# A ring of eight places: keeping the split weights of one token half for the other

## The chip, the cores and the metric

The kernel runs on one core of a Trainium2 chip. The metric is the device time of one execution, in microseconds (us). TensorE is called PE here, VectorE DVE, ScalarE ACT, GpSimd POOL, and SP is the engine that issues nearly all loads.

## The reference, cut to what matters

One token sequence (512 tokens, 1024 features, plus 256 context tokens later) goes through two layers of a first block and two layers of a second. Everything is float32. The change touches the first block, whose layer is

```
f = swiglu(modulate(x, sh1, sc1), ffn_in[l, 0], ffn_out[l, 0])
x = deepnorm_residual(x, f, g1, ln_g[l, 0], ln_b[l, 0], 0.5)
u = modulate(x, sh2, sc2)
m = even_mixer(u, ...)   # l = 0: RG-LRU and gated linear attention
m = odd_mixer(u, ...)    # l = 1: latent attention with low-rank q, k, v
x = deepnorm_residual(x, m, g2, ln_g[l, 1], ln_b[l, 1])
f = swiglu(modulate(x, sh3, sc3), ffn_in[l, 1], ffn_out[l, 1])
x = deepnorm_residual(x, f, g3, ln_g[l, 2], ln_b[l, 2], 0.5)
```

`deepnorm_residual` is a residual sum followed by a layer norm over the 1024 features of each token.

## The kernel before, in words

**Products.** Features lie on the partitions, tokens along the free axis. A weight matrix is cut into slabs: a slab is 128 output columns by up to 8 tiles of 128 input rows, 128 x 1024 numbers, 512 KB. For float32 accuracy each product is made of three: the weight is split into a high part (fp32r) and a low part (the rest), and so is the activation; PE adds high x high, high x low and low x high (L644 to L646), 24 matmuls for a slab. `class Lin` is one product (name, tensor, slabs, who makes the low parts), `SLABS` the list of all slabs in the order of use.

**The way of a slab.** SP loads it into one of `NRAW` = 3 raw places (`sp_slabs`, L526); it waits until the slab three before it has its low part. ACT copies it to the high part (`act_slabs`, L558). DVE ("v") or POOL ("g") subtracts to make the low part (`low_slabs`, L568); a name such as "vg" means by turns. High and low part lie in a split place (`halves`, L504): places 0, 1, 2 of 2048 words each, for some products also 3 and 4 (`place_slabs`, L215). A slab may be written to its place when the slab before it there (`before`) has had its last matmul (`release`).

**Token halves.** Where a product stands next to a layer norm, it is made in two passes, A for tokens 0 to 255 and B for tokens 256 to 511, so that the norm of one half runs beside the matmuls of the other. These are `gu` (l, f, 0, "A"/"B"), the first 8 slabs of `ffn_in`; `fo` (l, f, 1, A/B), the second half of `ffn_out`, whose slabs are in two parts (768 and 640 columns); `ob` and `oo`, the last products of the mixers, and `oi`, the first product of the odd mixer, of 4 slabs. Each pass loads and splits its slabs anew. gu(l, f) is used below for the pass pair of layer l, feed-forward f.

**Order.** Every engine's instructions are written out by a Python generator and run in that order. For output group m of a product, the engine first does the split work up to slab `ahead(m)` (L59), then its own work for m (`epilogue`): `act_linear`, `dve_linear`, `pool_linear` (L679 to L696). `ahead(m)` is the last slab whose place is free once the slabs before m have been used; with five places that is four slabs on. SP goes three further (`loads`).

**The seam between two passes.** In a tail pass (`fo`, `ob`, `oo`) DVE adds the residual for each m (L977), ACT squares it (L1071), POOL sums the tiles (L1048) and the squares (L1078). After the first slab of the next pass PE adds these sums over the partitions (`pe_ln`, L1098); DVE and ACT make mean and scale from them (`dve_ln` and `act_ln` at m = 0: L1149 to L1159, L1128), which stand in the queues behind the split work of m = 0; in the middle of its second slab PE spreads them over the partitions (`pe_ln_spread`, L1108). Then DVE normalizes two tiles per m (L1167, L1171, L1180), ACT writes the high part (L1131), DVE the low part (L1143) of the next product's input. At the start of `oo` ACT and POOL split the attention output (L1784, L1838).

Of the kernel before, what the change touches and what calls it, by code (L numbers as in the profile page):

```python
# [45 lines left out]
class Lin:  # L46


    def __init__(self, name, tensor, idx, mgs, kt, k0, mt, kch, split, low, toks):
# [4 lines left out]
        self.slab0 = 0  # L54
# [4 lines left out]
    def ahead(self, m):  # L59

        last, n = self.first(m) + len(self.cuts) - 1, self.first(m)

        def room(i):
            plain = i >= NRAW and not SLABS[i - NRAW].lin.split and i - NRAW >= last
            return not plain and (SLABS[i].before is None or SLABS[i].before < last)

        while n + 1 < len(SLABS) and room(n + 1):
            n += 1
        return n
# [54 lines left out]
def low_in(name):  # L124
    return {"B": "vg"}.get(name[-1], "v")
# [5 lines left out]

def weight_plan():
    out = []

    def lin(name, tensor, idx, mgs, kt=8, k0=0, mt=1, kch=8, split=True, low="v", toks=0):
        out.append(Lin(name, tensor, idx, mgs, kt, k0, mt, kch, split, low, toks))

    def ffn(l, f):
        for half in range(2):
            for name, tile0, cols in ffn_parts(l, f, half):  # L140
                n = 8 if len(name) > 4 else 22 - 2 * tile0
                lin(name, "ffn_in", (l, f), range(22 * half + 2 * tile0, 22 * half + 2 * tile0 + n), low=low_in(name))
# [23 lines left out]
    for name in ab("ob"):  # L166
        lin(name, "even_out", (), range(8), k0=8, low=low_out(name))
    ffn(0, 1)
    ffn(1, 0)
    for name in ab("oi"):  # L170
        lin(name, "odd_in", (), range(4), low=low_in(name))
# [4 lines left out]
    for name in ab("oo"):  # L176
        lin(name, "odd_out", (), range(8), low=low_out(name))
# [24 lines left out]
for _x in PLAN:  # L202
    _x.slab0 = len(SLABS)
# [10 lines left out]

def place_slabs():  # L215
# [3 lines left out]
    for n, s in enumerate(SLABS):  # L219
        if s.lin.split:  # L220
            more = [3, 4] if s.lin.name[0] in ("gu", "fo", "ob") or s.lin.name == ("oo", "B") else []
            ring = [0, 1, 2] + (more or ([5] if s.lin.name == ("glu", 0) else []))
            i = (i + 1) % len(ring)
            s.slot, s.before = ring[i], holds.get(ring[i])
            holds[ring[i]] = n
# [102 lines left out]
def _build(nc, a, out, ctx):  # L328
# [84 lines left out]
    scale_w = [ar(o, o + D) for o in SCALE_AT]  # L413
    HH, HL = rregion(F0, 11, 512)
# [89 lines left out]
    def halves(n):  # L504
        o, w = (SPL0, SPL0 + 2048, SPL0 + 4096, MORE0, MORE0 + 2048, E3)[SLABS[n].slot], SLABS[n].c1 - SLABS[n].c0
# [40 lines left out]
    def act_slabs(upto):  # L546
        while to_split["a"][0] <= min(upto, len(SLABS) - 1):
# [8 lines left out]
            if s.slot in (3, 4) and s.lin.name[0] == "ob":  # L556
                se.wait_ge(*(yield "p_gs", 3))
            se.activation(halves(n)[0], raw(n), ACT.Copy).then_inc(*sig("a_hi", n))  # L558
# [2575 lines left out]
```

## Time and profile before

| | us |
|---|---|
| median of 3 runs | 3929.87 (3925.76 to 3931.29) |
| the profiled execution | 3930.48 |
| its span | 3929.2 |
| PE busy | 3712.5 (94%) |
| DVE busy | 2164.7 (55%) |
| ACT busy | 1479.0 (38%) |
| POOL busy | 1082.3 (28%) |

The span is the time from the first to the last instruction of the profiled execution; the 1.3 us that the execution's own time is above it lie outside the program's instructions. Busy time of different engines overlaps. Times in the rows below are us from the span's start.

### The profile page before, as it was taken

How to read it: one execution, taken by the hardware profiler on the slowest of the kernel's cores; microseconds unless marked ns; L12 is line 12 of the kernel's file. 1: busy time of each engine (PE TensorE's matmuls, PEld its weight loads, DVE VectorE, ACT ScalarE, POOL GpSimd, SP SyncE). 2: the span in 40 equal slices, each digit the busy share in tenths (PEclk: the TensorE clock that was granted, in tenths of full speed). 3: DMA queues.
4: the chain of work that ended last, by engine and by line, in shares of the span. 5: the costliest groups of instructions: out<-in, count | busy, mean ns of one | idle time of the engine just before them, and what ended most of it. 6: DMA issues, size and time to landing. Idle time of an engine off the chain costs nothing.

```text
span 3929.2 us, 53436 instructions
## 1 busy us (share of the span) xinstructions
PE 3712.5 (94%) x21052; PEld 3105.7 (79%) x21052; DVE 2164.7 (55%) x3761; ACT 1479.0 (38%) x2556; POOL 1082.3 (28%) x753
## 2 busy tenths in 40 slices
PE   8999999899999999889999899899999989799999
PEld 7889878798889888659878777678778877677777
DVE  6555784675667776646333588821155338840442
ACT  3223554452235223444323423432235323353352
POOL 0003103251014102205201422933211423354224
PEclk9999999999999999998999899899999999899999
DMA  7565334345755565304332311012111212112112
GB/s 297 170 202 168 129 104 149 110 141 179 238 180 172 168 196 162 104 22 141 117 104 88 117 53 56 33 44 68 46 38 33 65 43 81 59 49 94 57 44 97
DMA packets 132153, 433.94 MB, mean 110 GB/s; under 512 B 14784, under 2 KB 14912, under 8 KB 131520
## 3 DMA queue, kind: packets, MB, share of 16 engines
q1 hardware_dynamic: 131904, 430.52, 33.8%
q8 instruction: 169, 2.77, 0.3%
q14 instruction: 80, 0.66, 0.1%
HBM read 428.36 MB, written 2.10 MB: 110 GB/s over the span
## 4 chain that ended last, share of the span: by engine, by line
PE 77%; DVE 11%; issue 5%; ACT 3%; POOL 3%; DMA 1%; SPq 0%; DVEq 0%; ACTq 0%; POOLq 0%
PE ps L644 21%; PE ps L646 21%; PE ps L645 21%; DVE cut L2287 4%; PE ps L1981 2%; POOL cut L568 1%; POOL cut L1048 1%; PE ps L1858 1%; PE ps L1942 1%; PE ps L1958 1%; PE ps L1964 1%; PE ps L642 1%; PE ps L1946 1%; DVE cut L568 1%; PE ps L670 1%
## 5 line engine op out<-in xcount | busy, mean ns | idle before, releaser
L644 PE MATMUL ps<-cut 128*128 128x512 f32 (+1 forms) x5312 | 1877.4, 353 | 88.9 <-DVE cut L2150 18.4
L645 PE MATMUL ps<-cut 128*128 128x512 f32 (+1 forms) x5312 | 1853.1, 349 | 0.0
L646 PE MATMUL ps<-cut 128*128 128x512 f32 (+1 forms) x5312 | 1851.8, 349 | 0.0
L644 PEld LDWEIGHTS ps<-cut 128*128 128x128 f32 x5312 | 1020.2, 192 | 245.6 <-issue 84.9
L645 PEld LDWEIGHTS ps<-cut 128*128 128x128 f32 x5312 | 1021.7, 192 | 127.6 <-issue 5.1
L646 PEld LDWEIGHTS ps<-cut 128*128 128x128 f32 x5312 | 1019.9, 192 | 126.8
L558 ACT ACTIVATE cut<-cut 128x1024 fp32r<-128x1024 f32 (+3 forms) x680 | 633.4, 939 | 840.7 <-PE ps L646 707.8
L568 POOL TENSOR_TENSOR cut<-cut 128x1024 fp32r<-128x1024 f32 (+3 forms) x266 | 580.9, 2186 | 1308.7 <-ACT cut L558 1308.3
L568 DVE TENSOR_TENSOR cut<-cut 128x1024 fp32r<-128x1024 f32 (+3 forms) x414 | 506.6, 1226 | 429.6 <-ACT cut L558 429.5
L945 POOL TENSOR_TENSOR cut<-cut 128x512 fp32r<-128x512 f32 (+1 forms) x100 | 143.8, 1438 | 1094.1 <-ACT cut L904 1094.1
L2287 DVE SCALAR_TENSOR_TENSOR cut<-cut,cols 128x512 f32<-128x512 f32 (+1 forms) x330 | 282.7, 857 | 11.7
L581 DVE CUSTOM_DVE_ANT_0 cut<-cut,cols 128x1024 f32<-128x1024 f32 x128 | 171.1, 1337 | 19.0 <-DMA cut<-in_mod_w 17.1
L926 DVE TENSOR_TENSOR cut<-cut,ps 128x512 f32<-128x512 f32 (+1 forms) x100 | 62.1, 621 | 186.3 <-PE ps L646 186.1
L2007 ACT ACTIVATE cut<-cut,st 128x512 f32<-128x512 f32 (+2 forms) x160 | 110.8, 694 | 137.6 <-DVE st L2040 137.5
L899 ACT ACTIVATE cut<-ps 128x512 f32<-128x512 f32 (+1 forms) x100 | 54.3, 543 | 271.4 <-PE ps L646 271.4
L2455 DVE TENSOR_TENSOR cut<-cut,ps 128x512 f32<-128x512 f32 (+1 forms) x48 | 28.0, 597 | 228.1 <-PE ps L646 228.1
L1048 POOL TENSOR_TENSOR cut<-cut 128x256 f32<-128x256 f32 x84 | 77.9, 927 | 153.1 <-DVE cut L977 153.1
L977 DVE SCALAR_TENSOR_TENSOR cut<-ps,deriv,cut 128x256 f32<-128x256 f32 (+1 forms) x144 | 81.5, 566 | 28.9 <-PE ps L646 28.9
L2299 POOL TENSOR_SCALAR const<-cut,cols 128x256 f32<-128x256 f32 x90 | 84.6, 940 | 8.6
L1981 PE MATMUL ps<-cut 128*64 128x128 f32 x1216 | 83.4, 280 | 0.7 <-DVE cut L2057 0.7
L904 ACT ACTIVATE cut<-cut 128x512 fp32r<-128x512 f32 (+1 forms) x100 | 56.8, 568 | 64.2 <-DVE cut L926 64.2
L589 DVE CUSTOM_DVE_ANT_0 cut<-cut,cols 128x1024 f32<-128x1024 f32 x48 | 79.7, 1661 | 1.7
(323 smaller groups left out, 3491.6 us busy)
## 6 DMA issues: line engine op xcount, KB each, us to landing
cut<-in_ffn_in SPq DMA_DIRECT2D x200, 512.0 KB, 4.1
cut<-in_mod_w SPq DMA_DIRECT2D x136, 512.0 KB, 4.4
cut<-in_ffn_out SPq DMA_DIRECT2D x96, 384.0 KB, 3.4
cut<-in_ffn_out SPq DMA_DIRECT2D x96, 320.0 KB, 3.2
cut<-in_w_ada SPq DMA_DIRECT2D x48, 512.0 KB, 3.5
cut<-in_w_merge SPq DMA_DIRECT2D x48, 512.0 KB, 3.5
cut<-in_even_in SPq DMA_DIRECT2D x36, 512.0 KB, 3.6
cut<-in_proj SPq DMA_DIRECT2D x48, 256.0 KB, 2.6
```

Source lines behind the costliest of these rows:

```text
L558: se.activation(halves(n)[0], raw(n), ACT.Copy).then_inc(*sig("a_hi", n))
L568: engine.tensor_tensor(lo, raw(n), hi.bitcast(F32), ALU.subtract).then_inc(*sig(which + "_lo", n))
L581: ve.tensor_tensor_reduce(junk, w, cb, 1.0, col("mod_b", 72 * l + i), ALU.mult, ALU.add, modc[:, 72 * l + i:72 * l + i + 1]).then_inc(*sig ...
L644: te.matmul(o, hi[:, k - ka, w], xs[0], start=k == 0, stop=False)
L645: te.matmul(o, hi[:, k - ka, w], xs[1], start=False, stop=False)
L646: ins = te.matmul(o, lo[:, k - ka, w], xs[0], start=False, stop=last)
L945: ge.tensor_tensor(HL[:, t, g[0]:g[1]], FTMP[t % 2][:, g[0]:g[1]], HH[:, t, g[0]:g[1]].bitcast(F32), ALU.subtract).then_inc(*sig("g_hl", g ...
L1048: ge.tensor_tensor(total, total if m > 1 else XA[:, 0, g[0]:g[1]], XA[:, m, g[0]:g[1]], ALU.add).then_inc(*sig("g_total", tag, part[-1], m))
L1981: ins = te.matmul(PS[b][64 * s:64 * s + 64, 0:128], J["v"][s][k], pbuf[:, s, k * 128:(k + 1) * 128], start=k == 0, stop=k == nv - 1)
L2007: se.activation(x, x, ACT.Exp, bias=stat(i, 1, s), accum_out=stat(i, 2, s)).then_inc(*sig("a_exp", tag, i, s))
L2287: ve.scalar_tensor_tensor(out=o, in0=x, scalar=c, in1=o, op0=ALU.mult, op1=ALU.add).then_inc(*sig("v_tap", l, t, h0, j))
L2299: ge.tensor_scalar(tmp, i, w, None, ALU.mult).then_inc(*sig("g_tmp", l, x, j))
```

## The change

B passes of `gu`, `ob`, `oi` and `oo` take the slabs of their A pass (`again`), which stay in their places until B has used them; they are not loaded or split a second time. So that a pass has room for 8 slabs, some lie in places beside the ring ("side"): free parts of the buffer at that time. The slabs in side places may be written when the last slab of the product before has been used (`before` = the slab ahead of the product's first). `oi` now has the ring of five, `oo` a ring of three and five side places, `gu` and `ob` a ring of five and three side places. During B a ring place comes free with each used slab, and the next product's slabs go there. The low parts of all these slabs are made by DVE. `fo` keeps its two passes as they were.

```diff
--- before.py
+++ after.py
@@ -46,12 +46,12 @@
 class Lin:
 
 
-    def __init__(self, name, tensor, idx, mgs, kt, k0, mt, kch, split, low, toks):
+    def __init__(self, name, tensor, idx, mgs, kt, k0, mt, kch, split, low, toks, again):
         self.name, self.tensor, self.idx, self.mgs, self.kt, self.k0 = name, tensor, idx, list(mgs), kt, k0
         self.mt, self.kch, self.split, self.low, self.toks = mt, kch, split, low, toks
         self.cuts = [(ka, min(kt, ka + kch)) for ka in range(0, kt, kch)]
         self.groups = len(self.mgs) * mt
-        self.slab0 = 0
+        self.slab0, self.again, self.stays = 0, again, False
 
     def first(self, m):
         return self.slab0 + (m // self.mt) * len(self.cuts)
@@ -59,10 +59,14 @@
     def ahead(self, m):
 
         last, n = self.first(m) + len(self.cuts) - 1, self.first(m)
+        end = self.slab0 + len(self.mgs) * len(self.cuts)
+        if self.again:
+            n = end - 1
 
         def room(i):
             plain = i >= NRAW and not SLABS[i - NRAW].lin.split and i - NRAW >= last
-            return not plain and (SLABS[i].before is None or SLABS[i].before < last)
+            freed = self.slab0 if self.stays and i >= end else last
+            return not plain and (SLABS[i].before is None or SLABS[i].before < freed)
 
         while n + 1 < len(SLABS) and room(n + 1):
             n += 1
@@ -122,24 +126,29 @@
 
 
 def low_in(name):
-    return {"B": "vg"}.get(name[-1], "v")
+    return "v"
 
 
 def low_out(name):
     return {"A": "v", "B": "gv"}.get(name[-1], "v")
 
 
+def first_of(name):
+
+    return name[:-1] + ("A",) if name[-1] == "B" else None
+
+
 def weight_plan():
     out = []
 
-    def lin(name, tensor, idx, mgs, kt=8, k0=0, mt=1, kch=8, split=True, low="v", toks=0):
-        out.append(Lin(name, tensor, idx, mgs, kt, k0, mt, kch, split, low, toks))
+    def lin(name, tensor, idx, mgs, kt=8, k0=0, mt=1, kch=8, split=True, low="v", toks=0, again=None):
+        out.append(Lin(name, tensor, idx, mgs, kt, k0, mt, kch, split, low, toks, again))
 
     def ffn(l, f):
         for half in range(2):
             for name, tile0, cols in ffn_parts(l, f, half):
                 n = 8 if len(name) > 4 else 22 - 2 * tile0
-                lin(name, "ffn_in", (l, f), range(22 * half + 2 * tile0, 22 * half + 2 * tile0 + n), low=low_in(name))
+                lin(name, "ffn_in", (l, f), range(22 * half + 2 * tile0, 22 * half + 2 * tile0 + n), low=low_in(name), again=first_of(name))
             for name in ([("fo", l, f, 0)], ab("fo", l, f, 1))[half]:
                 lin(name, "ffn_out", (l, f), range(8), kt=11, k0=11 * half, kch=6, low=low_out(name))
 
@@ -164,17 +173,17 @@
     for m in range(8):
         lin(("g", m), "even_in", (), [24 + m], low="g")
     for name in ab("ob"):
-        lin(name, "even_out", (), range(8), k0=8, low=low_out(name))
+        lin(name, "even_out", (), range(8), k0=8, again=first_of(name))
     ffn(0, 1)
     ffn(1, 0)
     for name in ab("oi"):
-        lin(name, "odd_in", (), range(4), low=low_in(name))
+        lin(name, "odd_in", (), range(4), low=low_in(name), again=first_of(name))
     lin(("qn",), "q_up", (), [0, 1], kt=2, mt=4, kch=2, split=False)
     lin(("qp",), "q_up", (), [2], kt=2, mt=4, kch=2, split=False)
     lin(("kn",), "kv_up", (), [0], kt=1, mt=8, kch=1, split=False)
     lin(("vu",), "kv_up", (), [1], kt=1, mt=8, kch=1, split=False, toks=4)
     for name in ab("oo"):
-        lin(name, "odd_out", (), range(8), low=low_out(name))
+        lin(name, "odd_out", (), range(8), again=first_of(name))
     ffn(1, 1)
     for l in range(2):
         lin(("glu", l), "w2_glu", (l,), range(8), low="g")
@@ -200,6 +209,11 @@
 LIN = {x.name: x for x in PLAN}
 SLABS = []
 for _x in PLAN:
+    if _x.again:
+        LIN[_x.again].stays, _x.slab0 = True, LIN[_x.again].slab0
+        for _i in range(len(_x.mgs)):
+            SLABS[_x.slab0 + _i].release = ("p_mm", _x.name, _i)
+        continue
     _x.slab0 = len(SLABS)
     for _i, _mg in enumerate(_x.mgs):
         for _p, (_ka, _kb) in enumerate(_x.cuts):
@@ -212,17 +226,28 @@
             SLABS.append(Slab(_x, _p, _mg, _ka, _kb, _end))
 
 
+SIDE = {"gu": (5, 6, 7), "ob": (8, 6, 5), "oo": (3, 4, 9, 10, 11)}
+
+
 def place_slabs():
 
 
     i, holds = -1, {}
     for n, s in enumerate(SLABS):
         if s.lin.split:
-            more = [3, 4] if s.lin.name[0] in ("gu", "fo", "ob") or s.lin.name == ("oo", "B") else []
-            ring = [0, 1, 2] + (more or ([5] if s.lin.name == ("glu", 0) else []))
-            i = (i + 1) % len(ring)
-            s.slot, s.before = ring[i], holds.get(ring[i])
-            holds[ring[i]] = n
+            name, j = s.lin.name, n - s.lin.slab0
+            side = SIDE.get(name[0], ()) if s.lin.stays else ()
+            nring = 8 - len(side)
+            if side and j >= nring:
+                s.slot, s.before = side[j - nring], s.lin.slab0 - 1
+            else:
+                more = [3, 4] if name[0] in ("gu", "fo", "ob", "oi") else []
+                ring = [0, 1, 2] + (more or ([5] if name == ("glu", 0) else []))
+                i = (i + 1) % len(ring)
+                s.slot, s.before = ring[i], holds.get(ring[i])
+            holds[s.slot] = n
+            if name == ("oo", "A") and j == 7:
+                i = SLABS[s.lin.slab0].slot - 1
 
 
 place_slabs()
@@ -411,6 +436,7 @@
     SCALE_AT = [F0 + 2 * D * t + D for t in range(6)] + [E3 + D, E3 + 2 * D]
     shift_w = [ar(o, o + D).rearrange("p (k m) -> p k m", k=8) for o in SHIFT_AT]
     scale_w = [ar(o, o + D) for o in SCALE_AT]
+    SLOTS = (SPL0, SPL0 + 2048, SPL0 + 4096, MORE0, MORE0 + 2048, E3, F0 + 2048, F0 + 7680, F0, F0 + 8192, F0 + 10240, F0 + 6144)
     HH, HL = rregion(F0, 11, 512)
     FTMP = [ar(F0 + 11264 + 512 * i, F0 + 11264 + 512 * (i + 1)) for i in range(4)]
 
@@ -502,7 +528,7 @@
         return ar(o, o + SLABS[n].c1 - SLABS[n].c0)
 
     def halves(n):
-        o, w = (SPL0, SPL0 + 2048, SPL0 + 4096, MORE0, MORE0 + 2048, E3)[SLABS[n].slot], SLABS[n].c1 - SLABS[n].c0
+        o, w = SLOTS[SLABS[n].slot], SLABS[n].c1 - SLABS[n].c0
         return rr(o, o + w), rr(o + 1024, o + 1024 + w)
 
     def tiles(n, v):
@@ -555,6 +581,9 @@
                 se.wait_ge(*(yield SLABS[s.before].release))
             if s.slot in (3, 4) and s.lin.name[0] == "ob":
                 se.wait_ge(*(yield "p_gs", 3))
+            if s.slot in (6, 8) and s.lin.name[0] == "ob":
+                se.wait_ge(*(yield "v_zl", 6))
+                se.wait_ge(*(yield "g_zl", 7))
             se.activation(halves(n)[0], raw(n), ACT.Copy).then_inc(*sig("a_hi", n))
 
     def low_slabs(which, engine, upto):
```

## Rows read from the trace of the kernel before

**Rows 1.** the page: span, engines (busy us, share, instructions), traffic, chain that ended last.

```profile
span 3929.2 us, 53436 instructions
...
PE 3712.5 (94%) x21052; PEld 3105.7 (79%) x21052; DVE 2164.7 (55%) x3761; ACT 1479.0 (38%) x2556; POOL 1082.3 (28%) x753
...
DMA packets 132153, 433.94 MB, mean 110 GB/s; under 512 B 14784, under 2 KB 14912, under 8 KB 131520
...
PE 77%; DVE 11%; issue 5%; ACT 3%; POOL 3%; DMA 1%; SPq 0%; DVEq 0%; ACTq 0%; POOLq 0%
```

**Rows 2.** PE's waits, 330 to 2220 us: total us, times, longest.

```profile
PE ps L1098 <- POOL cut L1078: 10.1, 4, 3.8
```

**Rows 3.** windows: stretch, length, busy us by engine, clock, DMA share, GB/s.

```profile
815.40:821.30 5.90, 5.79 (x50) 5.62 (x50) 2.57 (x10) 2.70 (x4) 2.36 (x1) 1.00 0.39 134
...
821.30:841.70 20.40, 20.35 (x170) 20.15 (x168) 20.10 (x41) 10.78 (x19) 11.29 (x9) 1.00 0.39 124
...
841.70:854.20 12.50, 8.74 (x48) 8.78 (x49) 5.03 (x12) 6.04 (x9) 4.29 (x5) 0.73 0.38 134
...
1221.90:1233.20 11.30, 8.73 (x49) 8.67 (x50) 6.03 (x13) 5.39 (x8) 2.35 (x2) 0.70 0.53 182
...
1600.70:1607.00 6.30, 5.76 (x50) 5.58 (x50) 2.99 (x11) 2.88 (x5) 0.72 (x1) 1.00 0.54 172
...
1612.90:1631.30 18.40, 14.50 (x96) 13.85 (x96) 12.04 (x24) 5.70 (x11) 5.32 (x2) 0.81 0.38 129
...
1802.40:1811.00 8.60, 7.16 (x49) 7.07 (x49) 3.52 (x12) 4.00 (x5) 4.47 (x3) 0.80 0.74 238
...
1831.40:1843.40 12.00, 8.68 (x48) 8.71 (x49) 5.31 (x13) 5.63 (x9) 3.85 (x5) 0.72 0.61 222
```

**Rows 4.** PE in time: start, us, line, operation [idle before, ended by].

```profile
845.46 2.85 PE L1098 MATMUL ps<-pick,cut 128*128 128x4 f32 x16 [3.80 <-POOL cut L1078]
...
851.51 1.79 PE L1108 MATMUL ps<-const,ln_st 128*128 128x128 f32 x8
...
1230.57 1.70 PE L1108 MATMUL ps<-const,ln_st 128*128 128x128 f32 x8
...
1616.91 0.39 PE L644 MATMUL ps<-cut 128*128 128x256 f32 x1 [2.00 <-DVE cut L1143]
...
1619.55 0.58 PE L644 MATMUL ps<-cut 128*128 128x256 f32 x1 [1.56 <-DVE cut L1143]
```

**Rows 5.** ACT in time: a slab's copy at the seam into gu(0,1).

```profile
845.72 1.04 ACT L558 ACTIVATE cut<-cut 128x1024 fp32r<-128x1024 f32 x1
```

**Rows 6.** slab subtractions from 821.3 to 849 us: count, busy us, mean ns.

```profile
L568 DVE TENSOR_TENSOR cut<-cut 128x1024 fp32r<-128x1024 f32 x7 | 9.1, 1299 | 3.4 <-ACT cut L558 3.4
...
L568 POOL TENSOR_TENSOR cut<-cut 128x1024 fp32r<-128x1024 f32 x1 | 2.4, 2417 | 0.0
```

**Rows 7.** DVE in time, at three seams.

```profile
843.09 1.64 DVE L568 TENSOR_TENSOR cut<-cut 128x1024 fp32r<-128x1024 f32 x1 [1.69 <-ACT cut L558]
...
844.65 0.47 DVE L977 SCALAR_TENSOR_TENSOR cut<-ps,deriv,cut 128x256 f32<-128x256 f32 x1
...
849.66 0.16 DVE L1159 TENSOR_TENSOR ln_st<-ln_st 128x2 f32<-128x2 f32 x1
...
1226.42 1.23 DVE L568 TENSOR_TENSOR cut<-cut 128x1024 fp32r<-128x1024 f32 x1 [1.43 <-ACT cut L558]
...
1771.42 1.75 DVE L568 TENSOR_TENSOR cut<-cut 128x1024 fp32r<-128x1024 f32 x1 [8.47 <-ACT cut L558]
```

**Rows 8.** POOL in time, at the end of ob/B and the start of oo/A.

```profile
837.60 2.32 POOL L1048 TENSOR_TENSOR cut<-cut 128x256 f32<-128x256 f32 x1 [2.29 <-DVE cut L977]
...
1765.88 10.87 POOL L1838 TENSOR_TENSOR cut<-cut 128x512 fp32r<-128x512 f32 x8 [140.78 <-ACT cut L1784]
...
1770.82 3.47 POOL L1838 TENSOR_TENSOR cut<-cut 128x512 fp32r<-128x512 f32 x2
```

**Rows 9.** DMA issue of gu(1,0)'s eighth slab, window 1227.5 to 1235 us.

```profile
cut<-in_ffn_in SPq DMA_DIRECT2D x1, 512.0 KB, 3.4
```

## The prediction

> **What bounds the kernel now.** I read the page first: PE is busy 3712.5 of 3929.2 us and holds 77% of the chain that ended last, DVE 11%, DMA 1% [rows 1]. So a removed copy is worth only the PE time that waited for it. I then asked for PE's waits in the stretch of the split products (330 to 2220 us) [rows 2], and for busy time and granted clock of each pass [rows 3]. Inside a pass PE hardly stops: seven slabs of the second half of `ob`, 821.3 to 841.7 us, show PE busy 20.35 of 20.40 us at clock 1.00 [rows 3]; a slab is 2.9 us. Lost time sits at seams, where PE waits for layer-norm sums: `L1098 <- POOL L1078`, 10.1 us in 4 waits [rows 2], and where oi/B waits for the low parts of normalized tiles (`L1143`, 2.00 and 1.56 us) [rows 4]. After each such wait the rows show half clock, 1.2 GHz: 0.73, 0.70, 0.80, 0.72 in the four seams, 0.81 in oi/B [rows 3]. The undisturbed seam (the sums, one slab, the spreading between its matmuls) is the row at 815.4: 5.9 us; each seam below is the same stretch.
>
> **What goes away.** 44 slabs (3 x 8 of `gu`, 8 `ob`, 8 `oo`, 4 `oi`) are no longer loaded and split again: 44 x 512 KB, 23.1 of 433.94 MB [rows 1]; 44 ACT copies of 1.04 us [rows 5], 46 us; 22 DVE subtractions at 1.3 us, 29 us, and 22 POOL ones at 2.4 us, 53 us [rows 6]. None is PE's, and full passes hide them; taken alone they are worth 0. The price lies in what the seams do. There are six terms; B before a seam means the second token half.
>
> **Term 1, end of ob/B into gu(0,1)/A.** Now the DVE is busy 20.10 of 20.40 us in the pass [rows 3], and makes seven slab subtractions up to 849 us [rows 6]. The last residual runs at 844.65, because DVE waited for the slab before it (843.09) [rows 7]; POOL is behind, one of its sums stretched to 2.32 us [rows 8]; PE waits 3.80 us, then sums and multiplies at half clock, and spreads at 851.51 [rows 4]. Afterwards ob/B makes five slabs (gu's first five, as their ring places come free at m=1 to 5) and none at m=6 and 7, so the last residual follows the one before it, at 840 to 841. POOL then has two totals and a square left, 0.7 us each: operands complete near 842.8, PE waits 1 us and not 3.8. But gu's places 5, 6, 7 come free only with ob's last matmul, and at m=0 of gu/A both ACT and DVE take them ahead of the statistics: three copies (1.0 each) from 842.5, the last subtraction ends near 846.7, and the statistics' chain of 1.5 us (from the end of PE's sums, 845.46 + 2.85 = 848.31 [rows 4], to 849.82 [rows 7]) gives the scale at 848.2. PE has been waiting there since 845.5, 2.7 us. The spread is 3.3 us earlier than 851.51. Behind it come 2.7 us now (half clock), 2.1 if the clock stays, some 4.2 if it drops again: -3.9 or -1.8. I take -3.0. Bounds: the seam down to 5.9 us, 12.5 - 5.9, -6.6; or 0.
>
> **Term 2, oo/A into oo/B:** 8.6 us now at clock 0.80 [rows 3]: POOL makes two oo/B slabs ahead of its last total. All lows are DVE's now and B has none, so POOL is on time as at 815.4, where the seam took 5.9: -2.7. Bounds -2.7 and 0.
>
> **Term 3, oo/B into gu(1,1)/A:** as term 1, from 12.0 us [rows 3]: -2.5; bounds -6.1 and 0.
>
> **Term 4, start of oo/A.** PE follows POOL's eight low parts of the attention output, 10.87 us; two of them took 3.47 while the DVE made one slab (1.75 us at 1771.42), the other six 1.23 each [rows 7, 8]: 1.0 us for one slab. At m=0 DVE now makes six slabs instead of one, two of them inside that stretch (the raws of the next three are there by then). +1.7; bounds 0 and +2.0. The Trainium skill (SBUF — State Buffer, Who interferes with whom) says that a `tensor_tensor` with both inputs in SBUF locks the port it shares with GpSimd, and that the later one fully blocks. The row agrees in kind; by the rule two whole subtractions would cost 2.5 us.
>
> **Term 5, fo(0,1,1)/B into gu(1,0)/A: a loss.** `fo` is not kept, so the seam stays late (11.3 us at 0.70 [rows 3]). At m=0 gu/A has one slab ahead of the statistics today, 1226.42 to 1227.65 [rows 7]; the change puts four there, since three side places are free. The eighth slab's load can be issued only then, when the fifth's low frees its raw place, and takes 3.4 us [rows 9]: it lands at 1231.1, is copied by 1232.1, subtracted by 1233.4, scale at 1234.9. PE gets to the spread at 1230.57 [rows 4]. +4.3, and a wait of this length has a half-clock stretch behind it (terms above), +1.5: +5.8. Bounds 0 (loads early enough) and +8.
>
> **Term 6, oi.** `oi` moves from a ring of three to five places, so its four slabs are made within the last two steps of fo(1,0,1)/B: two go ahead of residual 6, two ahead of residual 7. Today two in all are made there and the seam takes 6.3 us at clock 1.00; gu(1,0) has exactly the new order, 11.3 us at 0.70 [rows 3]. +5.0. Back comes this: two of DVE's normalizing steps lose the slab subtraction of 1.2 us ahead of them (part of it turns into waiting for ACT), so oi/B's first slab, 8.3 us now with its waits of 2.00 and 1.56 [rows 4], shrinks to 5.0, one wait of 2 us: -3.3, net +1.7. Bounds: all waits and the half clock in oi/B gone, 18.4 us to 3 x 2.9 + 2.9 (four slabs, 11.6), -6.8; or the whole seam lost and nothing back, +5.0.
>
> **At nothing:** loads and SP's order (raws of the next product come earlier, in DMA time that is free: 124 GB/s in the pass against 238 in a busy stretch [rows 3]); ob/A, where three more slabs ahead of residual 0 delay it by 6 us while eight banks of 2.9 us cover it; the extra waits of ACT for `v_zl` 6 and `g_zl` 7, which PE needs for the same slab anyway, with ob's first four slabs ready. If that cover is gone, ob/A would show 2 to 3 us of PE wait.
>
> **Sum:** -3.0 - 2.7 - 2.5 + 1.7 + 5.8 + 1.7 = +1.0 us. The profiled execution took 3930.48 us (span 3929.2); with +1.0 it is 3931.5, and the median of the runs lies 0.6 below it: **3931 us**.
>
> **Rivals.** (A) *The seams close:* the slabs ahead of the statistics find ACT and DVE idle and the removed work gives all that PE waited for. -6.6 - 2.7 - 6.1, terms 4 to 6 near 0: 3930 - 15.4 = 3915. For it: each of these waits names an engine that loses work. Against: copy, subtraction and statistics are one queue on each engine, and 1.0 and 1.2 us per slab are in the rows. (B) *Slabs ahead of the statistics decide,* slower: at m=0 of gu/A three or four slabs are made while PE has only 4.7 us of work before the spread; as soon as their chain is longer than that (more than two slabs, or one late load), the seam is as late as before, and half clock follows. Terms 1 and 3 at 0, 2 at -2.7, 4 +2, 5 +8, 6 +5: +12.3, 3942. For it: the 3.4 us load in term 5. Against: in terms 1 and 3 the raws are there. (C) *Nothing reaches PE:* copies go, the seams keep their lengths; the places serve but time stays, 3930. It would show as the same seam rows with 44 fewer loads.
>
> **Numbers.** Chances: forecast 0.53, A 0.22, B 0.20, C 0.05. A measurement here tells 0.2% (7.9 us) from no change. The forecast's own range is 3924 to 3938 and C lies in it; A is faster by over 0.2%, B slower, and the forecast's tails give each 0.02: faster 0.24, same 0.54, slower 0.22. The range takes in most of A and B: 3914 to 3941.
>
> **What would show it.** Right: seams at ob/B and oo/B 8 to 11 us long, with PE waiting at `L1108` for `ln_st`, no longer at `L1098`; gu(1,0)'s seam 15 us or more with the wait at `L1108`; oi's seam near 11 us; oo/A to oo/B 6 us; oo/A's first slab 12 us. Wrong: any wait of PE for `L568` inside a pass, seams of 6 us (A), or a seam at gu(0,1) still over 12 us (B).

## The result, and the profile after

Seven runs of the changed kernel have a median of 3939.92 us (3935.26 to 3944.63), seven of the kernel before on the same chip 3930.28 us. The ratio is 1.0021, 95% interval 1.0011 to 1.003: the change costs 8 us (4 to 12), where I had forecast 1. The profiled execution took 3936.43 us, 5.95 more than the one before [rows 1], so the traces show some 6 of the 8 us. They can be compared stretch by stretch: PE runs the same 21052 matmuls in the same order in both, so the same stretch is found by its first and last matmul.

In the changed kernel a line of the code is 29 further down: L673 to L675 are the products (before L644 to L646), L587 the slab's copy, L597 its subtraction, L1127 the sums over partitions, L1137 the spreading, L1172 the normalized low part. The page of after, for [rows 1]:

```profile
span 3935.2 us, 53263 instructions
...
PE 3705.5 (94%) x21052; PEld 3097.4 (79%) x21052; DVE 2121.1 (54%) x3739; ACT 1437.6 (37%) x2512; POOL 1013.8 (26%) x731
...
DMA packets 125816, 410.87 MB, mean 104 GB/s; under 512 B 14080, under 2 KB 14208, under 8 KB 125184
...
PE 75%; DVE 13%; issue 4%; ACT 3%; POOL 3%; DMA 2%; SPq 0%; DVEq 0%; ACTq 0%; POOLq 0%
```

All removed work is gone: 23.1 MB, 44 copies, 22 subtractions each of DVE and POOL; 7 us less of PE busy too. In the chain that ended last, PE lost two points and DVE gained two. The stretches of [rows 3] in the changed kernel (columns as there); the fifth is the start of oo/A, 13.0 us in the kernel before, and the last is a stretch of the second block:

```profile
840.96:851.73 10.77, 7.22 (x48) 7.07 (x49) 5.99 (x14) 5.71 (x9) 1.54 (x3) 0.86 0.46 147
1219.39:1237.00 17.61, 8.96 (x49) 8.64 (x50) 10.43 (x18) 7.93 (x12) 2.26 (x2) 0.73 0.62 205
1605.71:1614.87 9.16, 7.38 (x49) 7.20 (x50) 4.15 (x12) 1.56 (x5) 0.72 (x1) 0.81 0.42 148
1620.77:1634.64 13.87, 12.13 (x96) 11.47 (x95) 6.33 (x18) 3.60 (x8) 0.00 (x0) 1.00 0.07 20
1767.91:1782.87 14.96, 8.12 (x26) 6.09 (x27) 8.18 (x4) 9.69 (x14) 12.83 (x8) 0.58 0.30 94
1807.74:1813.20 5.46, 5.46 (x49) 5.46 (x49) 2.23 (x10) 1.24 (x2) 0.00 (x0) 1.00 0.01 3
1833.60:1843.65 10.05, 6.55 (x48) 6.40 (x49) 5.88 (x14) 5.61 (x8) 1.48 (x3) 0.92 0.80 278
2412.90:2432.55 19.65, 14.79 (x76) 9.17 (x74) 19.40 (x20) 7.09 (x16) 2.37 (x1) 0.74 0.08 27
```

The same last stretch in the kernel before:

```profile
2412.64:2425.99 13.35, 12.18 (x76) 8.34 (x74) 13.01 (x16) 7.09 (x16) 0.58 (x1) 1.00 0.12 39
```

Against [rows 3] this gives, in us:

| term | before | after | measured | forecast |
|---|---|---|---|---|
| 1, ob/B into gu(0,1) | 12.5 | 10.8 | -1.7 | -3.0 |
| 2, oo/A into oo/B | 8.6 | 5.5 | -3.1 | -2.7 |
| 3, oo/B into gu(1,1) | 12.0 | 10.1 | -1.9 | -2.5 |
| 4, start of oo/A | 13.0 | 15.0 | +2.0 | +1.7 |
| 5, seam into gu(1,0) | 11.3 | 17.6 | +6.3 | +5.8 |
| 6, oi: seam and oi/B | 6.3 + 18.4 | 9.2 + 13.9 | -1.7 | +1.7 |
| sum of the six | | | -0.1 | +1.0 |
| second block, from 2412.6 | 13.35 | 19.65 | +6.3 | none |

The six and the last row make +6.2, the undisturbed seam at 815.4 is 0.4 shorter, and everything else adds up to near nothing, though not in each part: PE's first 36 us are 3.6 shorter in this one profile, and the stretch from there to 753 us, ahead of every kept product, is 3.9 longer. So the six terms, all that the prediction priced, came out within some 1 us in their sum, and the loss lies 570 us behind the last of them.

Seams 1, 5 and 3 in the changed kernel, PE's sums and spreading in time (columns of [rows 4]):

```profile
841.96 1.92 PE L1127 MATMUL ps<-pick,cut 128*128 128x4 f32 x16 [1.05 <-POOL cut L1107]
...
848.33 1.05 PE L1137 MATMUL ps<-const,ln_st 128*128 128x128 f32 x5 [2.55 <-DVE ln_st L1188]
...
1233.22 2.04 PE L1137 MATMUL ps<-const,ln_st 128*128 128x128 f32 x8 [6.16 <-DVE ln_st L1188]
...
1840.91 1.13 PE L1137 MATMUL ps<-const,ln_st 128*128 128x128 f32 x8 [2.56 <-DVE ln_st L1188]
```

and what DVE and ACT did ahead of them:

```profile
842.23 2.94 ACT L587 ACTIVATE cut<-cut 128x1024 fp32r<-128x1024 f32 x3
...
843.30 3.50 DVE L597 TENSOR_TENSOR cut<-cut 128x1024 fp32r<-128x1024 f32 x3 [4.36 <-ACT cut L587]
...
848.02 0.16 DVE L1188 TENSOR_TENSOR ln_st<-ln_st 128x2 f32<-128x2 f32 x1
...
1226.50 1.06 ACT L587 ACTIVATE cut<-cut 128x1024 fp32r<-128x1024 f32 x1 [1.39 <-DMA cut<-in_ffn_in]
...
1229.38 1.06 ACT L587 ACTIVATE cut<-cut 128x1024 fp32r<-128x1024 f32 x1 [1.82 <-DMA cut<-in_ffn_in]
...
1232.92 0.16 DVE L1188 TENSOR_TENSOR ln_st<-ln_st 128x2 f32<-128x2 f32 x1
```

Read the first seam from the top: PE now waits 1.05 us and no longer 3.80 for the sums' operands; then three copies and three subtractions of gu's side places stand ahead of the statistics, which end at 848.18, and PE waits 2.55 us at the spreading. At gu(1,0) there are four, and ACT waits twice for a load that could be issued only late.

### The profile page after: what moved, and what is told of

It reads as the page before. It is cut to its first block, busy times and chain, and to the rows that moved or that the text cites. A ratio compares the mean times of both kernels' runs of the same rounds, so it can differ in the third digit from the quotient of the medians.

```text
span 3935.2 us, 53263 instructions
## 1 busy us (share of the span) xinstructions
PE 3705.5 (94%) x21052; PEld 3097.4 (79%) x21052; DVE 2121.1 (54%) x3739; ACT 1437.6 (37%) x2512; POOL 1013.8 (26%) x731
## 3 DMA queue, kind: packets, MB, share of 16 engines
q8 instruction: 169, 2.77, 0.3%
## 4 chain that ended last, share of the span: by engine, by line
PE 75%; DVE 13%; issue 4%; ACT 3%; POOL 3%; DMA 2%; SPq 0%; DVEq 0%; ACTq 0%; POOLq 0%
PE ps L673 20%; PE ps L674 20%; PE ps L675 20%; DVE cut L2316 6%; PE ps L2010 1%; POOL cut L1077 1%; DVE cut L597 1%; PE ps L1887 1%; POOL cut L597 1%; PE ps L1987 1%; PE ps L1971 1%; PE ps L671 1%; PE ps L1993 1%; PE ps L1975 1%; PE ps L699 1%
## 5 line engine op out<-in xcount | busy, mean ns | idle before, releaser
L673 PE MATMUL ps<-cut 128*128 128x512 f32 (+1 forms) x5312 | 1876.6, 353 | 90.1 <-DVE cut L2179 19.2
L675 PE MATMUL ps<-cut 128*128 128x512 f32 (+1 forms) x5312 | 1851.5, 349 | 0.0
L673 PEld LDWEIGHTS ps<-cut 128*128 128x128 f32 x5312 | 1019.2, 192 | 247.3 <-issue 84.7
L675 PEld LDWEIGHTS ps<-cut 128*128 128x128 f32 x5312 | 1018.9, 192 | 127.3
L587 ACT ACTIVATE cut<-cut 128x1024 fp32r<-128x1024 f32 (+2 forms) x636 | 586.9, 931 | 823.3 <-PE ps L675 699.6
L597 POOL TENSOR_TENSOR cut<-cut 128x1024 fp32r<-128x1024 f32 (+3 forms) x244 | 524.8, 2153 | 1289.3 <-ACT cut L587 1289.0
L597 DVE TENSOR_TENSOR cut<-cut 128x1024 fp32r<-128x1024 f32 (+3 forms) x392 | 469.0, 1201 | 427.6 <-ACT cut L587 427.5
L2316 DVE SCALAR_TENSOR_TENSOR cut<-cut,cols 128x512 f32<-128x512 f32 (+1 forms) x330 | 283.5, 859 | 11.7
```

What stands on the lines that cost most here:

```text
L597: engine.tensor_tensor(lo, raw(n), hi.bitcast(F32), ALU.subtract).then_inc(*sig(which + "_lo", n))
L673: te.matmul(o, hi[:, k - ka, w], xs[0], start=k == 0, stop=False)
L675: ins = te.matmul(o, lo[:, k - ka, w], xs[0], start=False, stop=last)
L2316: ve.scalar_tensor_tensor(out=o, in0=x, scalar=c, in1=o, op0=ALU.mult, op1=ALU.add).then_inc(*sig("v_tap", l, t, h0, j))
```

## The place of the 6.3 us: a shifted ring in the second block

Here PE waits for DVE's taps of a convolution (L2316, before L2287: 147 multiply-adds between 2230 and 2425 us) and the reciprocal behind them (L2240, before L2211). PE in the changed kernel:

```profile
2418.20 1.09 PE L2249 MATMUL ps<-cut,const 32*128 32x512 f32 x2 [0.93 <-DVE cut L2240]
2419.81 1.59 PE L2249 MATMUL ps<-cut,const 32*128 32x256 f32 x14 [0.52 <-DVE cut L2240]
2423.53 1.93 PE L2223 MATMUL ps<-cut,const 128*32 128x512 f32 x8 [2.12 <-DVE cut L2256]
2426.74 1.89 PE L2223 MATMUL ps<-cut,const 128*32 128x256 f32 x8 [1.28 <-DVE cut L2256]
```

In the kernel before only the last of these four waits is there, 1.17 us; the waits make 3.7 of the 6.3 us, half clock behind them the rest. DVE and POOL in the kernel before:

```profile
2318.70 2.50 DVE L2287 SCALAR_TENSOR_TENSOR cut<-cut,cols 128x256 f32<-128x256 f32 x1
...
2326.29 0.69 DVE L2740 TENSOR_TENSOR cut<-cut,ps 128x512 f32<-128x512 f32 x1 [1.51 <-ACT cut L2615]
...
2409.79 3.35 DVE L2211 RECIPROCAL cut<-cut 128x512 f32<-128x512 f32 x1
...
2318.43 5.03 POOL L568 TENSOR_TENSOR cut<-cut 128x1024 fp32r<-128x1024 f32 x2 [5.25 <-ACT cut L558]
...
2410.01 2.40 POOL L568 TENSOR_TENSOR cut<-cut 128x1024 fp32r<-128x1024 f32 x1 [6.20 <-ACT cut L558]
```

and in the changed one:

```profile
2326.53 0.69 DVE L2769 TENSOR_TENSOR cut<-cut,ps 128x512 f32<-128x512 f32 x1 [5.42 <-ACT cut L2644]
...
2327.59 3.01 DVE L2316 SCALAR_TENSOR_TENSOR cut<-cut,cols 128x256 f32<-128x256 f32 x2
...
2409.51 3.71 DVE L2316 SCALAR_TENSOR_TENSOR cut<-cut,cols 128x512 f32<-128x512 f32 x2
...
2414.71 4.96 DVE L2240 RECIPROCAL cut<-cut 128x512 f32<-128x512 f32 x2
...
2327.80 2.52 POOL L597 TENSOR_TENSOR cut<-cut 128x1024 fp32r<-128x1024 f32 x1 [14.26 <-ACT cut L587]
...
2410.27 2.40 POOL L597 TENSOR_TENSOR cut<-cut 128x1024 fp32r<-128x1024 f32 x1 [6.07 <-ACT cut L587]
```

A multiply-add that starts just after a POOL subtraction ends 0.3 to 0.6 us behind it: it takes 2.5 us and not 0.48 (2318.70 in the kernel before, where POOL's ends at 2320.9), 2.9 and not 0.75 (2410.30 in the changed one). It costs DVE 2.0 to 2.2 us. The Trainium skill (SBUF — State Buffer, "SBUF: two separate sides") describes this as an exclusive lock, taken by whichever starts first, against a DVE operation with two inputs in SBUF; the rows agree, and the reciprocal, which has one input, took 3.35 us beside POOL's subtraction as elsewhere.

The number of such holds is nearly the same, 14 in both; what changed is where they fall. In the kernel before three subtractions (at 2310.8, 2318.4 and 2320.9 us) lie before DVE's wait for ACT that ends at 2326.29, and that wait takes up their cost (1.51 us of it are left; 5.42 in the changed kernel, whose wait ends at 2326.53); in the changed kernel they run at 2302.0, 2311.0 and 2327.8. The third is behind the wait, and from there to the reciprocal DVE never pauses. And the one at 2410 hit the reciprocal before and hits a multiply-add now. These two holds are 4.2 of the 4.9 us by which the reciprocal starts later, at 2414.71 and not at 2409.79, and half clock follows PE's waits (0.74 against 1.00). The code says why. With 44 slabs fewer in the rings, the last slab of `fo(1,1,1)/B` lies in place 4 and not 3, so `glu(0)` takes places 1, 2, 5, 0 and not 0, 1, 2, 5; the first slabs of `nq(0)` behind it wait for other steps of `glu(0)` (the third for step 7, before for step 4), and POOL gets them at other times.

## The experiments

Each kernel was measured beside the kernel before, whose medians were 3929.4 (e1, e2, e4), 3932.8 (e5, e6, e7, e9), 3930.0 (e8, e10, e11) and 3933.2 us (e12); across these groups the ratios compare better than the times. Lines are two to four further down than in the changed kernel; those of e4_low are the lines of the kernel before.

| kernel | median us | ratio to before, 95% |
|---|---|---|
| e1_phase | 3929.1 | 0.9998 (0.9988 to 1.0007) |
| e2_cap | 3918.0 | 0.997 (0.9959 to 0.9982) |
| e4_low | 3931.3 | 1.0003 (0.9994 to 1.0011) |
| e5_cap_phase | 3911.0 | 0.994 (0.9926 to 0.9954) |
| e6_cap2 | 3911.0 | 0.9941 (0.9928 to 0.9955) |
| e7_cap_gu10 | 3922.5 | 0.9974 (0.9963 to 0.9985) |
| e9_cap_oi | 3929.9 | 0.9991 (0.9981 to 1.0) |
| e8_dose5 | 3915.8 | 0.9958 (0.9945 to 0.997) |
| e8_dose6 | 3919.7 | 0.9965 (0.9953 to 0.9977) |
| e11_nq_v | 3911.2 | 0.9945 (0.9933 to 0.9958) |
| e10_glu_v | 3902.0 | 0.9922 (0.991 to 0.9934) |
| e12_glu2 | 3894.6 | 0.9905 (0.9889 to 0.9922) |

**e1_phase: the ring set back.**

```diff
             name, j = s.lin.name, n - s.lin.slab0
+            if name == ("glu", 0) and j == 0:
+                i = -1
```

> The changed kernel with one line more in place_slabs: the ring's index is set back at glu(0)'s first slab, so that its slabs lie in places 0, 1, 2, 5 as before the change, and not in 1, 2, 5, 0. Theory (a shifted ring): the kept slabs stopped the ring in another phase, so two of glu(0)'s and the next slabs are made in other steps, POOL's subtractions fall beside other multiply-adds of DVE (L2316), which runs without a pause up to its reciprocal, and PE waits for that at 2416 to 2428 us; that is +5.0 of the +6.0 us between the two profiles. Then this kernel is 4 to 5 us faster than the changed one, 3935 us, and DVE's reciprocal starts near 2411 and not at 2414.71. Rival 1 (the lateness of the seams carries on): the reciprocal is late because PE came late to the stage; nothing changes, 3940 us. Rival 2 (chance of one profile, by the clock): nothing changes in the times, and the stretch differs at random.

Measured 3929.1 us, no longer to be told from the kernel before, and 6 us better than forecast. The stretch of 19.65 us is back at the 13.35 of the kernel before:

```profile
2412.18:2425.52 13.34, 12.17 (x76) 8.34 (x74) 12.98 (x16) 7.09 (x16) 0.58 (x1) 1.00 0.12 40
```

and the reciprocal starts at 2409.3 us (forecast 2411). POOL's subtractions run at 2310.3, 2318.0 and 2320.4, as before the change. Rivals 1 and 2 fall: the seams are as in the changed kernel. The four waits of PE stand in the two profiles with the shifted ring, the changed kernel's and e2_cap's (0.93, 0.52, 2.13, 1.28 there), and in none of the other twelve, each of which has the one wait of 1.17. The profiles differ by 6.4 us, of which this stretch is 6.3; the ratios differ by 9, and what the other 3 are no profile shows. PE's wait for the same reciprocal in the second layer is 14.1 us in the changed kernel and 11.7 here, but that is hardly time: PE comes to it 1.6 us later here, and the 560 matmuls around it take 139.4 and 138.8 us.

**e2_cap: no kept slab made early.**

```diff
-            return not plain and (SLABS[i].before is None or SLABS[i].before < freed)
+            x = SLABS[i].lin
+            near = not x.stays or i - last <= (2 if x.name[0] == "oi" else 4)
+            return near and not plain and (SLABS[i].before is None or SLABS[i].before < freed)
```

> The changed kernel, in which a slab of a product that keeps its slabs is made at most four slabs ahead of the one in use (two ahead for oi), as the rings of before had it; places, loads and copies are the same in number. Theory (slabs ahead of the statistics decide): the waits of PE at L1137 for ln_st go, in the seams gu(0,1) (2.7 us), gu(1,0) (6.2 us) and gu(1,1) (2.5 us), and oi's seam is as short as before (-3.8), while oi/B keeps its gain of 4.4: 2.7 + 6.6 + 2.2 + 3.8 = 15 us less than the changed kernel, 3925 us; each seam of gu 6 to 9 us. Rival (another chain): the statistics are late from their own inputs or the half clock follows any seam; then the seams keep 11 to 15 us and the time stays at 3940 us. Between: if only the late loads of gu(1,0) count, -6.6, 3933 us.

Measured 3918.0 (forecast 3925). The profile is 16.8 us under the changed kernel's, where 15 were forecast; by the ratios it is 20. Its stretches, in the order of terms 1, 5, 6 (two) and 3:

```profile
841.22:846.93 5.71, 5.55 (x47) 5.38 (x47) 2.90 (x10) 3.73 (x5) 0.13 (x1) 1.00 0.52 176
1214.82:1226.16 11.34, 8.77 (x49) 8.80 (x50) 5.02 (x13) 4.96 (x8) 3.11 (x3) 0.70 0.55 182
1594.03:1599.56 5.53, 5.53 (x50) 5.53 (x50) 3.03 (x10) 1.90 (x4) 0.00 (x0) 1.00 0.51 186
1605.45:1621.30 15.85, 13.46 (x97) 12.88 (x95) 6.92 (x20) 3.72 (x8) 0.00 (x0) 0.89 0.05 18
1820.25:1826.41 6.16, 5.80 (x48) 5.66 (x49) 2.87 (x10) 4.17 (x6) 0.60 (x1) 1.00 0.91 340
```

The two seams where the last slabs are kept close to the undisturbed length, 12.5 to 5.7 and 12.0 to 6.2 at full clock: -6.8 and -5.8 against the kernel before, the lower bounds of terms 1 and 3. Both waits of PE that the first seam had are gone, the 1.05 us for the sums and the 2.55 at the spreading (0.16 is left), so the slabs made early were what cost there. The seam into oi/A is as short as forecast (5.5), but oi/B keeps only half of its gain (15.9, and 13.9 in the changed kernel). The seam into gu(1,0) is what it was before the change, since `fo` is not kept.

A kernel that keeps all slabs but those of gu(1,0) (e3_gu10) would have priced term 5 alone. It has no time: with that edit PE, ACT and POOL wait for each other in a circle, and the expected 3933 us stay untried. e7_cap_gu10 below stands in for it.

**e8_dose5 and e8_dose6: one and two slabs more ahead** (the 4 of e6_cap2, below, turned to 5 and 6).

> As e6_cap2, but gu and ob may be five slabs ahead instead of four: one slab more stands ahead of the statistics at m=0 of each kept gu/A. Theory (a chain of 1.2 us per slab against PE's 4.7 us of cover; the prediction put the point at more than two slabs): two slabs are still covered in gu(0,1) and gu(1,1), PE's wait at the spreading stays under 0.5 us there; in gu(1,0) a load may be late, up to 1 us. So 3911 to 3913 us. Rival (any slab ahead of the statistics costs its full 1.2 us and the half clock behind it): +1.5 to 3 in each of three seams, 3916 to 3920 us.

> As e6_cap2, but gu and ob may be six slabs ahead: two slabs more ahead of the statistics. Theory: with three slabs the chain passes the cover by about 1.2 us in gu(0,1) and gu(1,1) (the changed kernel, with one more, showed 2.55), and in gu(1,0) the third waits for its load: 2.5 to 4 us and half clock behind. Sum +6 to +9 against e6_cap2: 3917 to 3920 us. Rival (cliff at the first slab): as e8_dose5 already, and here 3920 to 3925.

With five, DVE's subtractions between the last residual and the statistics of gu(0,1), and the spreading at gu(0,1) and gu(1,0):

```profile
841.32 1.23 DVE L601 TENSOR_TENSOR cut<-cut 128x1024 fp32r<-128x1024 f32 x1 [1.68 <-ACT cut L591]
...
844.08 1.13 PE L1141 MATMUL ps<-const,ln_st 128*128 128x128 f32 x8 [0.30 <-DVE ln_st L1192]
...
1223.15 1.13 PE L1141 MATMUL ps<-const,ln_st 128*128 128x128 f32 x8 [1.37 <-DVE ln_st L1192]
```

and the same with six:

```profile
847.67 2.36 DVE L601 TENSOR_TENSOR cut<-cut 128x1024 fp32r<-128x1024 f32 x2 [4.08 <-ACT cut L591]
...
851.57 1.13 PE L1141 MATMUL ps<-const,ln_st 128*128 128x128 f32 x8 [1.42 <-DVE ln_st L1192]
...
1231.53 1.84 PE L1141 MATMUL ps<-const,ln_st 128*128 128x128 f32 x7 [2.09 <-DVE ln_st L1192]
```

At gu(0,1) the slabs ahead of the statistics are not two with five and three with six, as the expectations have it. They are one with four and with five, two with six and three in the changed kernel: gu's first five go to ring places, and the fifth of them is made within ob/B when five are allowed. PE's wait at the spreading goes 0.16 (e2_cap) and 0.30 us with one slab, 1.42 with two, 2.55 with three, so 1.1 us for each slab from the second on. Rival B of the prediction and the expectation of e8_dose5 put the point at more than two slabs; it lies at one. PE reaches the spreading 3.8 us after it starts the sums (841.96 and 845.78 in the changed kernel), where the prediction gave it 4.7. At gu(1,0), with one, two, three and four slabs, the wait is nothing, 1.37, 2.09 and 6.16 us.

The times are 4.8 and 8.7 us over e6_cap2; for six slabs 6 to 9 had been forecast, for five 0 to 2. With five, one slab more of gu is made before the last residual of ob/B and oo/B, and PE waits 0.76 and 1.25 us for POOL's sums where four leave no wait. So one more slab can cost at the seam's other end. Only the seams show this, though: the two at gu(0,1) and gu(1,1) are 3.4 us longer than in e6_cap2, oi/B is 1.5 us shorter, the two profiles are equal in length (spans 3905.9 and 3906.5 us), and the intervals of the two ratios overlap.

**e7_cap_gu10 and e9_cap_oi: terms 5 and 6 alone** (e1_phase with the limit for gu(1,0), or for oi, only).

> e1_phase with the limit of four slabs ahead for gu(1,0) alone (term 5 alone). Theory: the seam from fo(0,1,1)/B loses PE's wait at the spreading (5.2 us in e1_phase) and its half clock, -6 to -7 us against e1_phase (3929.1), 3922 to 3923 us; all other seams as in e1_phase. Rival (a gain there is given back at the next seam by clock or waits): 3926 to 3929 us.

3922.5 us, 6.6 under e1_phase (9 by the ratios); its seam is 9.7 us where e1_phase has 16.7, and the other seams stay within 0.7 us. The term is real and its own. Of the 7.0 us some 1.6 are clock: the seam is as much shorter than the 11.3 of the kernel before and of e2_cap, at a granted clock of 0.82 and not 0.70.

> e1_phase with the limit of two slabs ahead for oi alone (term 6 alone). Theory: the seam from fo(1,0,1)/B is as short as before (-3.5 to -3.8), the gain in oi/B stays: 3925 to 3926 us. Rival: the wait moves into oi/A or oi/B, whose later slabs are then made in their way: 3929 us.

3929.9 us, no less than e1_phase. The seam closes from 10.3 us (e1_phase) to 5.5, but oi/B grows from 13.9 to 15.7, with half clock (0.89): 2.9 us net. The ratios differ by 2.8 us, within their intervals. Both theories are half right: a part moved.

**e4_low: the kernel before, with the low parts of gu's and oi's B passes by DVE.**

```diff
 def low_in(name):
-    return {"B": "vg"}.get(name[-1], "v")
+    return "v"
```

> The kernel before with one edit alone: the low parts of the B passes of gu, ob, oo, oi are all made by DVE; nothing is kept, all 44 slabs are loaded and split again. Theory A (the relief of POOL is the gain): ends of ob/B and oo/A and oo/B lose POOL's lateness as in the changed kernel, -2 to -3 us in each of three seams, 3923 us. Theory B (the relief works only where the second half makes no slabs): DVE, busy 20.10 of 20.40 us in ob/B, gets some four more subtractions of 1.3 us in a pass, and is late itself by 3 to 5 us at the end of ob/B, oo/B and the gu B passes: 3935 to 3945 us. I hold B likelier.

Neither: 3931.3 us, no difference. But the edit does less than the expectation says. `low_in` serves `gu` and `oi` alone; `ob` and `oo` take `low_out`, which it leaves as it was, and of POOL's 266 slab subtractions only 14 went to DVE. At the seam from oo/A into oo/B POOL still makes both slabs ahead of its last total, as in the kernel before (two, 5.71 us from 1798.75), and the seam is no shorter, 10.2 us for 8.6:

```profile
1796.98 2.42 POOL L568 TENSOR_TENSOR cut<-cut 128x1024 fp32r<-128x1024 f32 x1
1800.03 2.67 POOL L568 TENSOR_TENSOR cut<-cut 128x1024 fp32r<-128x1024 f32 x1 [0.62 <-ACT cut L558]
```

So the run shows that POOL's subtractions for the B passes of gu and oi cost nothing; what DVE's making those of ob and oo would give by itself, no run shows. That PE's wait at the end of ob/B is unchanged, 3.79 us against 3.80 [rows 4], is no answer either. The kernel before gives part of one: ahead of its total at 837.60 POOL stood idle for 2.29 us, waiting for DVE's residual [rows 8], and DVE's last subtraction waited 1.69 us for ACT's copy [rows 7]. At the end of ob/B the slabs of the pass's last steps were in the residual's way, and not POOL's own subtractions. In the changed kernel the edit of `low_in` by itself does nothing: the kept B passes make no slabs, and the A passes had "v" before.

**e5_cap_phase and e6_cap2: both edits; then oo too at most two ahead.**

> Both edits together: glu(0)'s slabs back in the places they had before (e1_phase) and no kept slab made more than four (oi: two) ahead of the one in use (e2_cap). Theory (two separate mechanisms, they add): e2_cap's profile is 17 us below the changed kernel's, of which the stretch at DVE's reciprocal still costs 4 to 5 us; so about 3913 us, 16 to 17 us under the kernel before. Rival (the gains share a cause, or the seams' earlier times shift DVE's chain by themselves): 3918 us, as e2_cap alone.

> As e5_cap_phase, with oo's slabs too made at most two ahead of the one in use. Theory (DVE's subtractions slow POOL's low parts of the attention output at the start of oo/A, term 4): fewer slabs are made beside those eight low parts, PE waits there as in the kernel before, -1.5 us, 3911 to 3912 us. Rival: oo/A, with fewer slabs ready, waits for a slab later; no gain, 3913 us or 1 to 2 us more.

3911.0 us for both. e5 shows that the two mechanisms add: 7 us below e2_cap and 18 below e1_phase. In ratios, e1 and e2 take 0.0023 and 0.0051 off the changed kernel's 1.0021, and e5 takes 0.0081. In e6 POOL's eight low parts take 10.86 us again, as in the kernel before [rows 8] (12.83 in the changed one), and the start of oo/A 13.0 and not 15.0 us; the times can't resolve these 2 us.

**e11_nq_v, e10_glu_v and e12_glu2: DVE makes what POOL made in the second block.**

```diff
-        lin(("glu", l), "w2_glu", (l,), range(8), low="g")
+        lin(("glu", l), "w2_glu", (l,), range(8), low="g" if l else "v")
```

This is e10; e11 has the same edit at `nq` and not at `glu`, e12 says "v" for both layers of `glu`. All else is e6_cap2.

> As e6_cap2, with the low parts of the four slabs of nq(0) made by DVE, not POOL. Theory (POOL's subtraction of 2.4 to 2.9 us holds the multiply-add of DVE that starts in it to its own end, 2.66 us instead of 0.75, so it takes 2.0 us from DVE's chain where that runs without a pause): a subtraction by DVE itself takes 1.2 and no multiply-add is held, DVE reaches its reciprocal 1.5 to 3 us earlier, PE's wait of 1.17 us behind it goes; 3910 us. Rival: the subtractions stand in DVE's queue behind multiply-adds, PE waits for a low part, and the time is 3913 to 3920 us.

3911.2 us: no gain. The reciprocal starts 7.2 us before PE's first matmul that needs it in e6 and 7.6 in e11; nq's holds had been taken up by DVE's wait, and the 1.17 us of PE don't depend on them.

> As e6_cap2, with the low parts of the eight slabs of glu(0) made by DVE. Same two theories as for nq: no held multiply-adds while glu(0) runs; DVE has waits for ACT in that stretch, which take up what is saved, so 3911 us, no change; rival: PE waits for low parts in glu(0), +2 to +8 us.

3902.0 us, 9 under e6_cap2 (7.5 by the ratios), where both theories had no gain. PE in e6_cap2 and in e10_glu_v, at the same matmul:

```profile
2271.71 0.58 PE L677 MATMUL ps<-cut 128*128 128x256 f32 x1 [4.51 <-DVE cut L2773]
```

```profile
2269.57 0.39 PE L677 MATMUL ps<-cut 128*128 128x256 f32 x1 [0.73 <-DVE cut L2773]
```

I had overlooked that within `glu(0)` PE waits for DVE's product L2773, which stands behind three held multiply-adds of 2.77 us. With DVE making the slabs they are gone and the wait is 3.8 us shorter; half clock (6.8 us in e6_cap2) no longer follows, and PE's stretch around it, 250 matmuls, takes 66.2 us and not 72.5. Some 3 us more come between 2470 and 2570. Why is not shown, and half of them are a stretch at 2550 us that takes 20.7 us in e6_cap2 and 18.9 here, but also 20.7 in the kernel before and 18.9 in the changed one.

> As e10_glu_v (3902 us, 28 us under the kernel before), with the low parts of glu(1)'s eight slabs made by DVE too. Theory (a POOL subtraction holds one multiply-add of DVE to its own end, 2.77 us instead of 0.75; a subtraction by DVE itself costs 1.22): in the second layer DVE runs without a pause from about 3265 us to its reciprocal, for which PE waits 11.7 us; the five or so slabs of glu(1) that lie in that stretch give 5 x 0.8 = 4 us, so PE's wait is 7 to 8 us and the time 3897 to 3899 us. Rival (the queue): DVE's subtractions stand behind multiply-adds, PE waits for a low part of glu(1) as long as is saved, and the time stays at 3902 us or rises.

3894.6 us, the best kernel here: 39 us under the kernel before, 1.0%. By the ratios it is 7 us under e10, where 3 to 5 were forecast. The forecast's place is the right one, though PE's wait for the reciprocal seems to say otherwise (11.71 us in e10, 14.07 in e12). The first reciprocal of that stretch in e10_glu_v:

```profile
3348.87 3.35 DVE L2244 RECIPROCAL cut<-cut 128x512 f32<-128x512 f32 x1
```

and in e12_glu2:

```profile
3343.14 3.35 DVE L2244 RECIPROCAL cut<-cut 128x512 f32<-128x512 f32 x1
```

Counted from the same matmul of PE (3228.25 and 3225.24 us) it comes 2.7 us earlier, and the whole stretch up to 3367 us is 3.0 us shorter: three subtractions moved in it, not five. PE itself comes to the wait 5.1 us earlier, since its three waits for low parts of glu(1)'s slabs went from 7.2 to 5.3 us and two half-clock stretches of 3.4 us went with them; the longer wait takes that up. Of the 6.4 us between the two profiles 2.7 lie in the first 1640 us, where the two kernels are the same.

## Why the prediction was right and wrong

**Where the bound lies.** Right: 23 MB and 153.5 us of busy time less (ACT 41.4, DVE 43.6, POOL 68.5, from the two pages; I had 128) gave PE nothing by themselves: between seams 1 and 5, with a whole B pass that makes no slabs for itself, PE takes 366.7 us in both kernels.

**Term 1.** The chain was right in kind and nearly in size: a wait of 1.05 for the operands (forecast 1), scale at 848.18 (848.2), PE's wait 2.55 (2.7). But the seam itself began 0.7 us earlier in the changed kernel (840.96, and 841.70 before), so counted from its start the spreading came 2.4 us earlier and not 3.3. Forecast was -3.9 or -1.8, by whether the clock stays. It fell, but for less long than forecast (3.4 us behind the spreading, not 4.2), and -1.7 was measured: that this meets -1.8 is two errors that cancel. Term 3 (-1.9) is the same case.

**Term 2.** Right (5.5 us, full clock); the seam of 5.9 us that I took as undisturbed was itself 0.4 long. The two slabs that POOL made ahead of its last total are gone, since B makes none; the other reason, "all lows are DVE's", was not needed for it and was not tried alone, as e4_low left oo's slabs as they were.

**Term 4.** Right: +2.0. POOL's eight low parts take 12.83 us and not 10.87 [rows 8], with three subtractions of DVE beside them in place of one: 1.0 us for each, as forecast.

**Term 5.** Right in mechanism: ACT waits for loads, PE for `ln_st`. PE waits 6.16 us, not 4.3. The seam began 2.5 us earlier than in the kernel before (1219.39, and 1221.90), which the forecast's times did not foresee; counted from its start, PE came to the spreading 1.0 us earlier than forecast (1227.1, and 1230.6 forecast) and the scale 0.7 us later (1233.1, and 1234.9). So the spreading moved by +5.2 us, not +4.3, and what stands behind it by +1.1, not +1.5: +6.3 for +5.8.

**Term 6.** Wrong in size: +2.9 and -4.5 for +5.0 and -3.3. No statistics were late there (PE waits 1.62 us for ACT's square, not at L1137), and in oi/B one wait of 1.69 us stayed as forecast, but the half clock went with the other (1.00). In e2_cap and e9_cap_oi, where a wait of 0.7 us stands ahead of one of the same length, half clock is back (0.89).

**The step that failed** is the list "at nothing" and where it ended. I priced loads and SP's order, and stopped at the last kept product. The rings go on through the whole kernel: taking slabs out turned the ring under `glu(0)`, which the diff doesn't touch. That was +6.3 us, and the rest of the kernel -0.3. That the measured 3940 us lies in the stated range of 3914 to 3941 is luck: the forecast's own range was 3924 to 3938, and the wider one reaches so far only to take in rival B. Nearly every sign that I had named for being right came true (oi's seam was 9.2 us for 11), and the time was 3940 and not 3931: the signs were all of seams. Rival B named a time, 3942, close to the measured one, for another reason: terms 1 and 3 did gain, and term 6 too. Rival A's two best terms were there to be had (-6.8, -5.8 in e2_cap), with the order changed. C is out.

## What to carry to other kernels

A buffer that comes free all at once lets a look-ahead rule put its refills in one heap ahead of whatever stands next in the queues; limit the look-ahead by need, not by room: the limit was worth 18 us (e1_phase to e5_cap_phase) where the reuse without it was worth none. When a change takes items out of a ring, list which later items change place and which step frees them, to the end of the program. Where DVE runs a long chain of operations with both inputs in SBUF, each POOL subtraction of 2.4 us beside it cost the chain 2.0 us or a little more here; it was free ahead of a wait of DVE, and DVE doing the work itself can be cheaper (1.22 against 2.0 us). A longer wait of PE is no loss by itself: see what PE waits for, and whether that came later or PE came earlier.

## What the runs showed of the hardware

A `TENSOR_SCALAR` of DVE is held by POOL as well, though it has one input, and the reciprocal is not; e10_glu_v, DVE and POOL:

```profile
2283.31 2.21 DVE L2317 TENSOR_SCALAR cut<-cut,cols 128x256 f32<-128x256 f32 x1
...
2282.98 2.40 POOL L601 TENSOR_TENSOR cut<-cut 128x1024 fp32r<-128x1024 f32 x1 [79.93 <-ACT cut L591]
```

It takes 0.41 us undisturbed. POOL is hardly stretched, 2.40. The cost comes in steps of a whole hold, as at 2410 us above, where a subtraction that fell beside the reciprocal cost nothing and beside a multiply-add 2.2 us. Not every step is time: PE's wait for the second layer's reciprocal was 11.7 us in nine of the kernels and 13.8 to 14.1 in five (before, after, e2, e11, e12), but in the first four of the five PE had come to it 1.6 us earlier, with one half-clock stretch less, and the stretch as a whole was only 0.5 us longer (139.3 to 139.4 us, and 138.9).
